# Turning the query and key tiles of a hybrid decoder layer by 32x32 block transposes on VectorE and a round trip through DRAM instead of on TensorE

## The reference

```python
q = rope(rms_norm(qkv[:, :, :, 0], q_norm), cos, sin)   # 3 groups x 4 heads x 128
k = rope(rms_norm(qkv[:, :, :, 1], k_norm), cos, sin)
for g, (window, dilation) in enumerate(((128, 1), (512, 4), (2048, 16))):
    o_g, lse_g = dilated_window_attention(q[:, :, g], k[:, :, g], v[:, :, g], window, dilation)
wts = softmax(stack(lses)); att = sum(wts * stack(outs))
```

## Time and profile before

| What | Value |
|---|---|
| Median of 3 runs | 1344.43 us (1344.31 to 1344.99) |
| Span of the profiled execution, first to last instruction | 1342.2 us |
| TensorE busy | 1331.9 us (99%) |
| VectorE busy | 781.2 us (58%) |
| GpSimd busy | 531.0 us (40%) |
| ScalarE busy | 507.8 us (38%) |
| DMA | 139.51 MB, 84823 packets, 104 GB/s mean |
| Mean granted TensorE clock | 0.999 of full |

### The profile page before, as it was taken

One profiled execution on the slowest core, in us unless ns is written; L12 is line 12 of the kernel. 1 busy time (PEld: TensorE's weight loads), 2 busy tenths in 40 slices (PEclk: granted clock), 3 DMA queues, 4 the chain that ended last, 5 costly groups with the idle time before them and its releaser, 6 DMA issues.

```text
span 1342.2 us, 17647 instructions
## 1 busy us (share of the span) xinstructions
PE 1331.9 (99%) x6262; PEld 1104.3 (82%) x6262; DVE 781.2 (58%) x1253; ACT 507.8 (38%) x1282; POOL 531.0 (40%) x500
## 2 busy tenths in 40 slices
PE   9999999999999999999999999999999999999998
PEld 6887888888888888888888888888888888888887
DVE  6799887842779666565665752148512566134323
ACT  7455646542434444344443688311200011223100
POOL 6975424404458334041340632342067317044020
PEclk9999999999999999999999999999999999999999
DMA  6232312322203032120320332376279644122111
GB/s 240 79 102 87 109 56 79 110 100 72 75 12 84 24 92 64 31 83 22 97 58 30 114 98 88 100 237 220 94 275 412 198 126 157 55 79 63 40 47 47
DMA packets 84823, 139.51 MB, mean 104 GB/s; under 512 B 10464, under 2 KB 41472, under 8 KB 84736
## 3 DMA queue, kind: packets, MB, share of 16 engines
q10 hardware_dynamic: 40288, 75.82, 16.0%
q1 hardware_dynamic: 44448, 62.56, 15.6%
HBM read 108.84 MB, written 29.51 MB: 103 GB/s over the span
## 4 chain that ended last, share of the span: by engine, by line
PE 92%; DVE 5%; issue 1%; ACT 1%; DMA 0%; POOL 0%; SPq 0%; POOLq 0%; DVEq 0%; ACTq 0%
PE bank L1275 28%; PE bank L1280 28%; PE bank L1279 28%; PE bank L1432 2%; PE bank L1412 2%; PE bank L1399 1%; PE bank L1421 1%; DVE xc L1012 1%; PE bank L1525 1%; PE bank L1320 0%; DMA gain_mix<-in_gain_mix 0%; ACT L750 0%; DVE ibuf L1039 0%; DVE qkr L1116 0%; DVE ibuf L1028 0%
## 5 line engine op out<-in xcount | busy, mean ns | idle before, releaser
L549 POOL TENSOR_TENSOR ring<-raw,ring 128x512 fp32r<-128x512 f32 x221 | 310.5, 1405 | 727.1 <-PE bank L1280 642.8
L1275 PE MATMUL bank<-hn,ring 128*128 128x512 f32 x640 | 251.8, 393 | 1.4 <-DVE sgbuf L1000 1.2
L1280 PE MATMUL bank<-hn,ring 128*128 128x512 f32 x640 | 249.4, 390 | 0.0
L1279 PE MATMUL bank<-hn,ring 128*128 128x512 f32 x640 | 249.2, 389 | 0.0
L1275 PE MATMUL bank<-ring,hn 128*128 128x512 f32 x576 | 232.6, 404 | 0.2 <-POOL ring L549 0.2
L1280 PE MATMUL bank<-ring,hn 128*128 128x512 f32 x576 | 225.8, 392 | 0.0
L1279 PE MATMUL bank<-ring,hn 128*128 128x512 f32 x576 | 225.2, 391 | 0.0
L553 POOL TENSOR_SCALAR ring<-raw 128x512 fp32r<-128x512 f32 x221 | 183.5, 830 | 7.9 <-DMA raw<-in_w_rnn_s 7.8
L1275 PEld LDWEIGHTS bank<-hn,ring 128*128 128x128 f32 x640 | 120.2, 188 | 26.7 <-DVE sgbuf L1000 1.6
L1280 PEld LDWEIGHTS bank<-hn,ring 128*128 128x128 f32 x640 | 120.1, 188 | 25.3
L1279 PEld LDWEIGHTS bank<-hn,ring 128*128 128x128 f32 x640 | 120.3, 188 | 24.0
(11 more groups left out here) (181 smaller groups left out, 2153.7 us busy)
## 6 DMA issues: line engine op xcount, KB each, us to landing
raw<-in_w_tail_s SPq DMA_DIRECT2D x104, 256.0 KB, 2.7
g_in<-gate_dram ACTq DMA_DIRECT2D x48, 256.0 KB, 4.4
raw<-in_w_rnn_s SPq DMA_DIRECT2D x45, 256.0 KB, 2.6
raw<-in_w_qkv_s SPq DMA_DIRECT2D x48, 192.0 KB, 2.5
gate_dram<-g_out ACTq DMA_DIRECT2D x32, 256.0 KB, 2.1
raw<-in_w_qkv_s SPq DMA_DIRECT2D x48, 128.0 KB, 2.2
o_dram<-o_buf ACTq DMA_DIRECT2D x48, 128.0 KB, 1.8
o_in<-o_dram ACTq DMA_DIRECT2D x12, 512.0 KB, 3.5
```

The source lines that it names most:

```text
L549: nc.gpsimd.tensor_tensor(ring[:, ring_slot(p), 1], raw[:, p % RAW], ring[:, ring_slot(p), 0].bitcast(F32), ALU.subtract).then_inc(w_ready, 1)
L1275: ins = T.matmul(out, lhs[0], rhs[0], start=first, stop=False)
L1279: T.matmul(out, lhs[0], rhs[1], start=False, stop=False)
L1280: return T.matmul(out, lhs[1], rhs[0], start=False, stop=last)
```

## The change

The two transposes on PE, ACT's copy of them and bank 4's use in the steps go. In their place DVE writes the rotated tile into `qkn` and turns each 32x32 block of it into `qkr` (one `transpose` of 128x256). SP then sends `qkr` to a DRAM buffer of 4 places in four DMAs, one for each 32 partitions, in runs of 32 elements (128 bytes), waits for them, and reads the whole tile back into `qkT` in one DMA of 512-byte runs. The blocks change places on the way, so that the tile arrives fully turned. SP walks `MAIN_ORDER` too: the weight loads are issued in fixed portions between the tiles (`loaded_after`), where before each was issued as soon as its `raw` buffer was free. GpSimd now runs `lo_part(p - 1)` ahead of the waits for piece p. DVE waits for its own last turn before it writes `qkn` again, and for `turn_out` before it writes `qkr`.

```diff
--- before.py
+++ after.py
@@ -33,6 +33,8 @@
 SCALE = float(HD) ** -0.5
 MASKED = -1.0e30
 CLASSES = (1, 4, 8)
+QUAD = 32
+QUADS = P // QUAD
 
 OFF_Z_RNN = RNN
 OFF_QKV = 2 * RNN
@@ -87,7 +89,7 @@
 START = [("norm", t) for t in range(4)] + [("hn", n) for n in range(6)] + [("norm", 4), ("hn", 6), ("hn", 7)] \
     + [("norm", t) for t in range(5, NT)] + [("hn", n) for n in range(KD, 2 * KD)]
 
-LAG_T, LAG_QK, LAG_ET, LAG_PV = 2, 4, 5, 6
+LAG_QK, LAG_ET, LAG_PV = 4, 5, 6
 STEPS = TILES + LAG_PV
 FIRST_STEP, STEP_BLOCKS = 90, 6
 STEP_AT = {FIRST_STEP + STEP_BLOCKS * A: A for A in range(STEPS)}
@@ -105,6 +107,16 @@
 
 
 MAIN_ORDER = main_order()
+
+
+def loaded_after(G):
+
+    if G < SLOTS_Q:
+        c, s = divmod(G, NT)
+        return FIRST_QKV + KD * (c + 1) + (0 if s < 1 else KD // 2 if s < 3 else KD)
+    return FIRST_TAIL + max(KD, G - SLOTS_Q + 11)
+
+
 Q_STAT = 15
 
 P_CUT = (2, 4)
@@ -339,6 +351,7 @@
         y_dram = nc.dram_tensor("y_dram", (NJ, 2, P, S), F32, kind="Internal").ap()
         o_dram = nc.dram_tensor("o_dram", (UNITS, P, S), F32, kind="Internal").ap()
         gate_dram = nc.dram_tensor("gate_dram", (2 * KD, P, S), F32, kind="Internal").ap()
+        turn_dram = nc.dram_tensor("turn_dram", (4, 2 * QUADS, QUAD, QUADS, QUAD), F32, kind="Internal").ap()
         stat_dram = nc.dram_tensor("stat_dram", (2, TILES, P), F32, kind="Internal").ap()
         mw_dram = nc.dram_tensor("mw_dram", (GROUPS, HEADS * NT, P), F32, kind="Internal").ap()
 
@@ -394,8 +407,8 @@
         sq_done = sem("sq_done")
         std_done = sem("std_done")
         qkr_done = sem("qkr_done")
-        tq_done = sem("tq_done")
-        qkT_done = sem("qkT_done")
+        turn_out = [sem("turn_out0"), sem("turn_out1")]
+        qkT_in = [sem("qkT_in0"), sem("qkT_in1")]
         qk_done = sem("qk_done")
         max_done = sem("max_done")
         exp_done = sem("exp_done")
@@ -501,17 +514,48 @@
                 sp.dma_start(dst[:], a[src]).then_inc(chan_in, 16)
             sp.dma_start(spare_first[:, :, 0], chunk_bias(0).rearrange("p (q i) -> p q i", q=4)).then_inc(bq_in[0], 16)
 
-            for p in range(RAW, PIECES):
-                sp.wait_ge(w_ready, p + 1 - RAW)
...
+            def load_pieces(first, end):
+
+                for p in range(first, end):
+                    sp.wait_ge(w_ready, p + 1 - RAW)
...
+                return max(first, end)
+
+            def turn_tile(g):
+
+                r, s = g % 2, g % NT
+                squares = turn_dram[g % 4]
+                sp.wait_ge(qkr_done, g + 1)
+                if g >= 4:
+                    sp.wait_ge(qkT_in[r], 16 * ((g - 4) // 2 + 1))
+                for i in range(QUADS):
+                    sp.dma_start(squares[:, :, i].rearrange("b i j -> i b j"),
+                                 qkr[i * QUAD:(i + 1) * QUAD, r].rearrange("p w a b -> p (w a b)").rearrange(
+                                     "p (b j) -> p b j", j=QUAD)).then_inc(turn_out[r], 16)
+                sp.wait_ge(turn_out[r], 16 * QUADS * (g // 2 + 1))
+                if g >= NT:
+                    old = g - NT
+                    sp.wait_ge(qk_done, old - old % NT + last_reader(old // (HEADS * NT), old % NT) + 1)
+                sp.dma_start(qkT[:, :, s * P:(s + 1) * P],
+                             squares.rearrange("(w b) i a j -> (b i) w (a j)", w=2)).then_inc(qkT_in[r], 16)
+
+            loaded = load_pieces(RAW, FIRST_QKV + KD)
+            for what, G in MAIN_ORDER:
+                if what == "slot":
+                    loaded = load_pieces(loaded, loaded_after(G))
+                elif G < TILES:
+                    turn_tile(G)
+                if (what, G) == ("step", TILES - 1):
+                    break
+            load_pieces(loaded, PIECES)
 
 
         @block.gpsimd
@@ -569,6 +613,8 @@
                     nc.gpsimd.tensor_scalar(dst, src, 1.0, 1.0, ALU.mult, ALU.mult).then_inc(perm_done, 1)
 
             for p in range(PIECES):
+                if p >= 1:
+                    lo_part(p - 1)
                 if p in PERM_PIECE:
                     permute_hn(PERM_PIECE[p])
                 pool.wait_ge(raw_in[p % RAW], raw_count(p))
@@ -576,8 +622,6 @@
                     pool.wait_ge(w_used, slot_before(p) + 1)
                 if p == FIRST_O:
                     pool.wait_ge(pv_done, TILES)
-                if p >= 1:
-                    lo_part(p - 1)
                 if p == SOFTPLUS_AT:
                     softplus()
                 hi_part(p)
@@ -731,16 +775,6 @@
                             load_gains(2, 1)
                     if r == 1 and 1 <= g < GROUPS:
                         negate_sin(g, half)
-                g = A - LAG_T
-                if 0 <= g < TILES:
-                    act.wait_ge(tq_done, g + 1)
-                    if g >= NT:
-                        old = g - NT
-                        act.wait_ge(qk_done, old - old % NT + last_reader(old // (HEADS * NT), old % NT) + 1)
-                    s = g % NT
-                    nc.scalar.activation(qkT[:, :, s * P:(s + 1) * P],
-                                         bank[4][:, 0:2 * P].rearrange("p (w q) -> p w q", w=2),
-                                         ACT.Copy).then_inc(qkT_done, 1)
                 g = A - LAG_QK
                 if 0 <= g < TILES:
                     grp, tile = g // (HEADS * NT), g % NT
@@ -1102,6 +1136,8 @@
                     if u % HEADS == 0 and s % (NT // 2) == 0:
                         dve.wait_ge(cs_neg[s // (NT // 2)], grp + 1)
                         dve.wait_ge(gq_in, 16 if grp < 2 else 32)
+                    if g >= 1:
+                        dve.wait_ge(qkr_done, g)
                     for w in range(2):
                         c, b = part_of(u, w)
                         ins = V.scalar_tensor_tensor(qkn[:, w].rearrange("p a b -> p (a b)"),
@@ -1109,13 +1145,15 @@
                                                      gain_qk[:, grp % 2, w], ALU.mult, ALU.mult)
                     link(ins)
                     if g >= 2:
-                        dve.wait_ge(tq_done, g - 1)
+                        dve.wait_ge(turn_out[g % 2], 16 * QUADS * (g // 2))
                     rot = qkr[:, g % 2]
                     cs4 = cossin[:, s, 0].unsqueeze(1).unsqueeze(1).to_broadcast([P, 2, 2, HD // 2])
                     sn4 = cossin[:, s, 1:3].unsqueeze(1).to_broadcast([P, 2, 2, HD // 2])
                     V.tensor_tensor(rot, qkn[:], cs4, ALU.mult)
                     link(V.tensor_tensor(qks[:, :, ::-1], qkn[:], sn4, ALU.mult))
-                    V.tensor_tensor(rot, rot, qks[:], ALU.add).then_inc(qkr_done, 1)
+                    link(V.tensor_tensor(qkn[:], rot, qks[:], ALU.add))
+                    V.transpose(rot.rearrange("p w a b -> p (w a b)"), qkn[:].rearrange("p w a b -> p (w a b)")
+                                ).then_inc(qkr_done, 1)
 
             for what, G in MAIN_ORDER:
                 if what == "step":
@@ -1388,22 +1426,13 @@
 
 
             def attention(A):
-                g = A - LAG_T
-                if 0 <= g < TILES:
-                    if g == 0:
-                        pe.wait_ge(rg_read, 2 * NJ)
-                    pe.wait_ge(qkr_done, g + 1)
-                    if g >= 1:
-                        pe.wait_ge(qkT_done, g)
-                    for w in range(2):
-                        ins = T.transpose(bank[4][:, w * P:(w + 1) * P],
-                                          qkr[:, g % 2, w].rearrange("p a b -> p (a b)"), ident[:])
-                    ins.then_inc(tq_done, 1)
                 g = A - LAG_QK
                 if 0 <= g < TILES:
                     grp, tile = g // (HEADS * NT), g % NT
                     prev = has_prev(grp, tile)
-                    pe.wait_ge(qkT_done, g + 1)
+                    if g == 0:
+                        pe.wait_ge(rg_read, 2 * NJ)
+                    pe.wait_ge(qkT_in[g % 2], 16 * (g // 2 + 1))
                     if g >= 1:
                         pe.wait_ge(max_done, g)
                     keys = qkT[:, 1, (prev_tile(grp, tile) if prev and grp == 0 else tile) * P:(tile + 1) * P]
@@ -1475,7 +1504,6 @@
                 if q == Q_STAT:
                     pe.wait_ge(max_done, TILES)
                     pe.wait_ge(exp_done, TILES)
-                    pe.wait_ge(qkT_done, TILES)
                     for w, st in enumerate((neg_max, den)):
                         T.transpose(bank[4][0:TILES, w * P:(w + 1) * P], st[:], ident[:]).then_inc(statT_done, 1)
 
```

18 lines of the change are left out of this document (9 added, 9 removed).

## The result

The changed kernel takes 1356.56 us (median of 4 runs, 1350.27 to 1358.15) against 1344.71 for the kernel before in the same comparison (4 runs): a ratio of 1.0079, 95% interval 1.0057 to 1.0101. It is 12 us **slower**, where 1327.6 was forecast, and outside the range of 1321 to 1348. Its four runs lie 7.9 us apart, so a difference against this kernel is known to some 3 us only.

A forecast was written before the change was run, and what follows sets the result against it. TensorE, busy for 99% of the span, was taken as the bound: 1344.4 - 20.2 for the removed transposes + 3.4 for VectorE's stalls = 1327.6 us, all other terms 0; range 1321 to 1348.

The forecast's parts named there:

- TensorE's term: Attention steps: removing 96 transpose pairs at 0.21 us each saves 20.2 us, all on the chain.
- The transpose: VectorE's 128x256 block transpose in each attention step: taken as 0.42 us, plus 0.05 for a semaphore hop.
- The second rival: VectorE's transpose is held up beside GpSimd, 1.27 us for 0.42: 1332.7 us, or 1349 if nothing is free; chance 0.12.
- SP's write landings: SP's writes of each turned tile to DRAM: land in 1.8 us, with ends of 1.7 and 4.6.
- 3.3 was forecast: SP's time per tile for four write issues, landing, read issue and two semaphore hops: 3.3 us, cost 0.
- the first rival: SP becomes the bound if its writes land late: 1344.4 us at a landing of 3.12, 1486 at 4.6; chance 0.16.
- The weight load of the score product: Third rival: with the transposes gone this load stands bare on TensorE, giving back up to 0.21 us a step; chance 0.05.
- each piece still has at least four slots (27 us) before its first use ... Both 0: Weight loads in fixed places and GpSimd's low part moved ahead: pieces arrive in time, so both cost 0.
- the term of 3.4 us for VectorE: VectorE's added transposes cost 3.4 us in all, beside GpSimd's two permutations, and 0 elsewhere.
- about 2 us are free: At each GpSimd permutation VectorE falls 4.5 us behind; about 2 are free and 2.5 are paid, twice.
- I expect no change: TensorE's granted clock stays at 1.00, the level of 2.4 GHz, in all of the attention.
- 0.9 was forecast for the packets: DMA engines' time for a tile's 1024 short and 256 longer packets: 0.9 us of a step.

The follow-up runs named there:

- x6_perm_first: Changed kernel with GpSimd's second permutation ahead of the four late weight pieces, and those pieces two slots later in SP's order: 1343.29 us.
- x14_perm_back: x10_copies_first with the second permutation and the weight portions put back as in the changed kernel: 1338.62 us.
- x2_portions: Kernel before, transposes still on TensorE, with only the weight loads in fixed portions and GpSimd's low part moved ahead: 1359.03 us.
- x3_extra_turn: Kernel before with VectorE's block transpose added for each tile, into a buffer nobody reads: 1352.68 us.
- x12_perm_no_turn: x6_perm_first without VectorE's block transpose: 1336.98 us.
- x4_no_turn: Changed kernel without VectorE's block transpose, tiles going out unturned inside their 32x32 blocks: 1347.86 us.
- x10_copies_first: x6_perm_first with probabilities' transposes and product with v one step later, SP's read after the next tile's send, ScalarE's copies ahead of its exponential: 1327.43 us.
- x11_before_copies: Kernel before, transposes on TensorE, with the longer distance to the probabilities' transposes and ScalarE's copies ahead of its exponential: 1341.30 us.
- x1_early: Changed kernel with the first half of the next chunk's weight pieces loaded after slot 0 instead of slot 1: 1349.59 us.

## Why the prediction was wrong

**Right.** TensorE's term: 96 x 0.21 = 20.2 was forecast, 0.22 a step measured. The transpose: 0.42 assumed, 0.445 measured, and 448 ns at most, so it is not held up beside GpSimd (0.45 at 448.67, in the permutation, right behind a two-input pass of 1.19). The second rival falls by that. The Trainium skill (SBUF — State Buffer, Who interferes with whom) names only passes with two SBUF inputs or in a two-port mode as held up; the trace agrees, with the number just given. SP's write landings: 1.8 us median forecast and measured, with longest 4.4. SP took a median of 3.85 us for a tile where 3.3 was forecast, mostly in issuing, and kept up on the mean; the first rival, to which I gave nearly all of the chance of "slower", is not what happened. The Trainium skill (DMA: Bandwidth & Descriptors, Specifications) has the DMA engines read, modify and write under 512 bytes. In the landings of 1.8 us no price of that is to be seen. The weight load of the score product did not come out bare.

**The step that failed first** is "each piece still has at least four slots (27 us) before its first use ... Both 0". It measured the pieces against TensorE, which uses them, and not against GpSimd, which cuts them in a fixed order with a permutation behind them. TensorE never waited for a piece; it waited for what stood behind the pieces in GpSimd's queue. Measured: 13.3 us (`x6_perm_first`), 11.2 (`x14_perm_back`), and 14.4 for the loads and the low part alone, of which 9.5 are steps 18 and 19 (`x2_portions`), instead of 0. What was needed was at hand: the permutation's place in GpSimd's program, in front of which the diff puts a load that comes later.

**The second** is the term of 3.4 us for VectorE. I costed it at the two permutations, with "about 2 us are free" at each, and counted 0 beside the cuts of the nine chunks. Measured: 8.1 us for the pass alone (`x3_extra_turn`, TensorE at its old pace) and 6.3 with the permutation moved (`x12_perm_no_turn`). In the changed kernel seven chunk ends besides step 14 lose 11.9. Only 4.4 of these go with the transpose: `x4_no_turn` still loses 7.5 there, and `x2_portions`, with the transposes on TensorE, loses 4.6 at the same steps. What was missing is ScalarE. At a chunk's end it waits for VectorE, then loads two tables of 1.28 us each, and only then takes the exponential that TensorE reads at the distance of the changed kernel. A step further off TensorE no longer needs this exponential, but a copy stands behind it in the same queue, and VectorE's delay passes on to a reader that has nothing to do with it. With the distance and the order both changed (`x10_copies_first`) none of the seven steps loses 0.4 us. That the changed kernel, with all its parts, is 12 us slower and not 14.4 + 8.1 - 20.2 = 2.3 says that the parts don't add. The likely reason, not shown by itself, is that a TensorE that is 0.2 us a step faster has less slack for the same lateness.

**The third** is "I expect no change" of the granted clock. It held wherever TensorE did not wait. Windows of 5 us over the attention add up to 10 us of clock missing in the changed kernel (each window's length times what its clock lacks of 1.00), and to 0 in the kernel before, in `x11_before_copies` and in `x10_copies_first`. How much of the 10 is time is not settled: between 446 and 454 TensorE would have waited for GpSimd anyway. The four runs of the changed kernel say that it is not little. The one with a mean clock of 0.996 has a span of 1348.3 us, the others, at 0.990 to 0.992, 1353.5 to 1356.0. So most of the 7.9 us between them goes with the clock, though these four numbers don't tell whether the clock made the waits dearer or longer waits lowered the clock. At 0.996 the kernel is still 5.6 us slower than before. For one step the price can be read off (below).

That `x10_copies_first` takes 1327.4 us, beside a forecast of 1327.6, is chance. It has another distance and another order of ScalarE, worth 3.2 us on the kernel before, and still loses time that the forecast did not count.

**Left open.** The split of steps 18 and 19 between waiting and the lower clock; why the longer distance alone slows the kernel before by 3.6 us, for which I have only the argument of ScalarE's order; and the losses that remain in `x10_copies_first` beside the second permutation (steps 12 to 16, 5.5 us).

## What to carry to other kernels

When loads are moved to fixed places in a queue, follow each one to the engine that consumes it and on to whatever stands behind it in that engine's program: a deadline can belong to the next work item, not to the piece. When an engine gets a little slower, ask of every reader of the engines behind it whether it waits for that result or only for something queued after it. Reordering such a queue gave 13.7 us here, but only with the reader moved a step further off; each of the two alone gave 1 us or cost time. And a saving on the bounding engine is only worth its sum if the slack of all the others is measured against the shorter step.

## What the runs showed of the hardware

**The same wait, with and without a fall of the clock.** In step 57 TensorE waits 1.8 us for the copy in both the changed kernel and `x1_early`. In the changed kernel:

```profile
660.00:665.00 5.00, 4.23 (x14) 3.57 (x15) 1.92 (x6) 2.80 (x15) 0.00 (x0) 0.66 0.65 158
```

In `x1_early`:

```profile
651.20:656.20 5.00, 3.22 (x18) 2.70 (x17) 3.06 (x9) 4.04 (x16) 0.00 (x0) 1.00 0.52 149
```

The step loses 3.62 us in the first and 2.07 in the second, 1.55 less. So of two equal waits one was followed by a fall of the clock to 1.2 GHz and the other was not; why is not shown.

**Runs of 128 bytes landed no later than long ones.** 384 transfers of 256 such runs, 116448 packets under 512 bytes in all against 10464 before, landed in 1.8 us at the median while the queue also loaded weights; the landing of those weight loads rose from 2.3 us to 2.7. The queue's share of the 16 DMA engines' time rose from 15.6% to 24.3%, which is 1.2 us of their time for each tile, where 0.9 was forecast for the packets.

**An issue takes longer in a row.** The four writes of a tile were issued in 1.78 to 2.90 us, 1.89 at the median, and a single one in 0.444 (302 to 1452 ns), where I had taken 0.33 from single loads. From the first write's issue to the end of the read's, a tile took SP 3.37 to 6.20 us, 3.85 at the median.
